# Seven pairs of steps instead of four, down products two steps behind, one of the block sums made by a transfer that adds

## What is computed

```python
def _swiglu(x, w_gate, w_up, w_down):
    return (jax.nn.silu(x @ w_gate) * (x @ w_up)) @ w_down

for l in range(2):
    x = x + 0.5 * _swiglu(_rmsnorm(x, ffn1_norm[l]), ffn1_w_gate[l], ffn1_w_up[l], ffn1_w_down[l])
    ...   # the mixer
    x = x + 0.5 * _swiglu(_rmsnorm(x, ffn2_norm[l]), ffn2_w_gate[l], ffn2_w_up[l], ffn2_w_down[l])
```

## Time and profile before

| | |
|---|---|
| runs, us | 1147.65, 1147.89, 1147.91 (median 1147.89) |
| the profiled execution | 1147.37 us, its span 1145.6 |
| granted TensorE clock | 0.999 of full speed |
| TensorE busy | 99% of the span |
| VectorE busy | 81% |
| ScalarE busy | 54% |
| POOL busy | 18% |

### The profile page before, as it was taken

One profiled execution on the slowest core, in us unless ns is written; L12 is line 12 of the kernel. 1 busy time (PEld: TensorE's weight loads), 2 busy tenths in 40 slices (PEclk: granted clock), 3 DMA queues, 4 the chain that ended last, 5 costly groups with the idle time before them and its releaser, 6 DMA issues.

```text
span 1145.6 us, 15668 instructions
## 1 busy us (share of the span) xinstructions
PE 1137.4 (99%) x5477; PEld 932.3 (81%) x5477; DVE 927.9 (81%) x1434; ACT 615.3 (54%) x789; POOL 211.7 (18%) x413
## 2 busy tenths in 40 slices
PE   9999999999999999999999999999999999999997
PEld 7888888888777888888888888888877788888886
DVE  6878886878987687789788788867898695988895
ACT  6455645457764454455454555454677635454453
POOL 2221230062000012121301221302510000122221
PEclk9999999999999999999999999999999999999999
DMA  8976575795325578756659756647953435886552
GB/s 296 312 265 209 165 232 167 239 263 193 125 75 184 184 233 268 260 164 223 205 194 298 256 175 224 207 154 216 274 164 108 141 136 183 284 283 217 162 196 103
DMA packets 168080, 235.82 MB, mean 206 GB/s; under 512 B 17376, under 2 KB 112848, under 8 KB 168016
## 3 DMA queue, kind: packets, MB, share of 16 engines
q1 hardware_dynamic: 146720, 222.23, 59.0%
q0 software_dynamic: 11008, 8.80, 3.2%
q10 hardware_dynamic: 10288, 4.00, 1.4%
HBM read 221.86 MB, written 1.05 MB: 195 GB/s over the span
## 4 chain that ended last, share of the span: by engine, by line
PE 99%; DVE 1%; issue 0%; ACT 0%; POOLq 0%; POOL 0%; DVEq 0%
PE ps L1645 28%; PE ps L1647 28%; PE ps L1646 28%; PE ps L1778 2%; PE ps L1779 2%; PE ps L1777 2%; PE ps L1903 2%; PE ps L1959 2%; PE ps L1931 2%; PE ps L1695 1%; PE ps L1664 1%; DVE wlo L639 0%; PE ps L1874 0%; PE ps L2082 0%; PE ps L1990 0%; PE ps L1950 0%
## 5 line engine op out<-in xcount | busy, mean ns | idle before, releaser
L639 DVE TENSOR_TENSOR wlo<-raw,whi 128x2048 fp32r<-128x2048 f32 (+2 forms) x195 | 427.5, 2198 | 80.5 <-ACT whi L1347 54.0
L1347 ACT ACTIVATE whi<-raw 128x2048 fp32r<-128x2048 f32 (+2 forms) x195 | 359.2, 1843 | 206.4 <-PE ps L1647 160.2
L1645 PE MATMUL ps<-whi,ht_hi 128*128 128x512 f32 (+1 forms) x1064 | 415.8, 391 | 0.6 <-DVE wlo L639 0.6
L1647 PE MATMUL ps<-whi,ht_lo 128*128 128x512 f32 (+1 forms) x1064 | 411.0, 386 | 0.0
L1646 PE MATMUL ps<-wlo,ht_hi 128*128 128x512 f32 (+1 forms) x1064 | 410.5, 386 | 0.0
L1645 PEld LDWEIGHTS ps<-whi,ht_hi 128*128 128x128 f32 x1064 | 199.9, 188 | 40.9 <-ACT whi L1347 1.0
L1647 PEld LDWEIGHTS ps<-whi,ht_lo 128*128 128x128 f32 x1064 | 199.8, 188 | 40.9
L1646 PEld LDWEIGHTS ps<-wlo,ht_hi 128*128 128x128 f32 x1064 | 200.1, 188 | 38.6
L536 POOL DMA_DIRECT2D act_blocks<-act_blocks x224 | 110.0, 499 | 458.0 <-DVE act_blocks L709 458.0
L1645 PE MATMUL ps<-whi,at_hi 128*128 128x512 f32 x304 | 118.5, 390 | 0.0
L1646 PE MATMUL ps<-wlo,at_hi 128*128 128x512 f32 x304 | 118.3, 389 | 0.0
(11 more groups left out here) (235 smaller groups left out, 1266.9 us busy)
## 6 DMA issues: line engine op xcount, KB each, us to landing
raw<-in_ffn_w_down_dram SPq DMA_DIRECT2D x88, 512.0 KB, 4.4
raw<-in_w_in_dram SPq DMA_DIRECT2D x88, 512.0 KB, 4.6
raw<-in_ffn_w_gate_dram SPq DMA_DIRECT2D x77, 512.0 KB, 4.0
raw<-in_ffn_w_up_dram SPq DMA_DIRECT2D x77, 512.0 KB, 5.0
T_raw<-in_ffn_w_gate_dram SPq DMA_DIRECT2D x16, 512.0 KB, 5.8
T_raw<-in_ffn_w_up_dram SPq DMA_DIRECT2D x16, 512.0 KB, 5.9
raw<-in_w_out_dram SPq DMA_DIRECT2D x16, 512.0 KB, 4.3
raw<-in_ffn_w_gate_dram SPq DMA_DIRECT2D x19, 256.0 KB, 2.9
```

Of the source, the lines that this page charges most:

```text
L639: nc.vector.tensor_tensor(wlo[:, n, 0:w], raw[:, n, 0:w], whi[:, n, 0:w].bitcast(F32), ALU.subtract).then_inc(lo_done, 1)
L1347: nc.scalar.activation(whi[:, n, 0:w], raw[:, n, 0:w], ACT.Copy).then_inc(hi_done, 1)
L1645: nc.tensor.matmul(o, xh, wh, start=start, stop=False)
L1647: return nc.tensor.matmul(o, xl, wh, start=False, stop=stop)
```

## The change

- **Pairs.** (0,0) has one pair, at step 8; the other three FFNs have two, at steps 4 and 8. An FFN's order of blocks is now made by `ffn_plan`: gate a, gate b of a step, then the down blocks of all steps up to two before it; a pair is b11, T2, b21, b22, T4 in the ring of blocks, and T3 and T1 from buffers of their own.
- **Two steps behind.** The down product of step i - 2 follows the gate blocks of step i. Activations alternate between at and bt, step banks between 0 and 2.
- **Sums.** T3, T1 and T2 are made by VectorE (`sum_of`), T4 by a transfer issued by POOL that adds T2 into T4's buffer (`add_part`). T2 and T4 are rounded straight into the ring (`convert_sum`). With p0 the FFN's first pair, T3 and T1 are summed in step p0 - 4 ahead of its products, T2 after them, together with `side_full`, which adds the halves of the normed x; `side_sums` (four instead of ten) follow in step p0 - 3. For a second pair the sums stand behind the first.
- **Turning.** Step 0 is turned as every other step. In steps 0 to 7 all twelve transfers are issued by POOL, and the four quadrants that stay are copied by ScalarE (`keep_act`) instead of transposed a second time by VectorE. PE's own turn of the first FFN is gone.
- **Loads.** The parts for the first pair are loaded with the blocks of steps p0 - 4 and p0 - 3; for the second with b22, 6a, 6b and down 2.
- **Loops** of PE and POOL are written out.

The core of the diff:

```diff
+PAIRED = {(0, 0): (8,), (0, 1): (4, 8), (1, 0): (4, 8), (1, 1): (4, 8)}
+def ffn_plan(l, f):
+    plan, waiting = [], []
+    for i, pair in ffn_steps(l, f):
+        if pair:
+            plan += [("b11", i), ("T2", i), ("b21", i), ("b22", i), ("T4", i)]
+            waiting += [i, i + 1]
+            continue
+        plan += [("gate", i, 0), ("gate", i, 1)] + [("down", j) for j in waiting if j <= i - 2]
+        waiting = [j for j in waiting if j > i - 2] + [i]
+    return plan + [("down", j) for j in waiting]
...
 # VectorE
+            def side_full(l, f):
+                nc.vector.tensor_tensor(full, ht_hi[:, :, :].bitcast(F32), ht_lo[:, :, :].bitcast(F32), ALU.add)\
+                    .then_inc(side_sum, 1)
...
+                nc.vector.tensor_tensor(sum_raw[name][:, :], sum_raw[first][:, :], sum_raw[second][:, :], ALU.subtract)\
+                    .then_inc(part_sub, 1)
...
+                p0 = PAIRED[l, f][0]
                 dve.wait_ge(rstd_ready, (l * 3 + n) * 3 + 3)
+                for n, key in enumerate(FFN_PLAN[l, f][:-2]):
+                    kind, i = key[:2]
+                    if kind == "b11":
+                        paired(l, f, i)
+                    if kind == "gate" and key[2] == 1:
+                        products(l, f, i)
+                        if l == f == i == 0:
+                            convert(l, s0 + 3)
+                        if not behind_pair(l, f, i):
+                            turn_product(l, f, i)
+                        convert_next(l, f, s0 + n + 3)
+                        if i == p0 - 4:
+                            sum_of(l, f, p0, "T2")
+                            side_full(l, f)
+                        if i + 2 in PAIRED[l, f][1:]:
+                            sum_of(l, f, i + 2, "T3")
+                    if kind == "gate" and key[2] == 0:
+                        if i and not behind_pair(l, f, i):
+                            convert_next(l, f, s0 + n + 3)
+                        if i == p0 - 4:
+                            sum_of(l, f, p0, "T3")
+                            sum_of(l, f, p0, "T1")
+                        if i == 2:
+                            act_rest(l, f, 0)
+                        if i == p0 - 3:
+                            side_sums(l, f)
+                        if i == p0 - 1:
+                            side_rest(l, f)
+                    if kind == "down":
+                        k = rounded_behind(l, f, i)
+                        if k == NSTEP - 1 or k == NSTEP - 2:
+                            act_rest(l, f, k)
+                        convert_next(l, f, s0 + n + 3)
+                        if k is not None and k < NSTEP - 2:
+                            act_rest(l, f, k)
...
 # POOL
+            def add_part(l, f, p):
+                z = PAIR_NUMBER[l, f, p]
+                pool.wait_ge(part_in["T4"], (z + 1) * 32)
+                pool.wait_ge(part_sub, z * 3 + 3)
+                apart(pool)
+                pool.dma_start(sum_raw["T4"][:, :], sum_raw["T2"][:, :], accum_op=ALU.add).then_inc(part_added, 16)
...
 # ScalarE
+            def keep_act(l, f, i):
+                eng.wait_ge(act_turned, (l * 2 + f) * NSTEP + i + 1)
+                blocks_in, blocks_out = act_set(i)
+                for q in range(4):
+                    nc.scalar.activation(blocks_out[32 * q:32 * q + 32, P * q:P * q + P],
+                                         blocks_in[32 * q:32 * q + 32, P * q:P * q + P], ACT.Copy)\
+                        .then_inc(act_kept_early, 1)
...
 # PE
+                product(1, quadrant(halves, 0, 0), from_ring(at("b11", p), 4), True).then_inc(slab_used, 1)
+                pe.wait_ge(side_l, r + 1)
+                product(0, s3, from_sums("T3"), True).then_inc(pair_ps, 1)
+                product(3, s2, from_ring(at("T2", p), 4), True).then_inc(slab_used, 1)
+                product(2, s1, from_sums("T1"), True).then_inc(pair_ps, 1)
...
-                with pe.Fori(2, PAIR) as i:
-                    gate_up(l, f, i)
-                    down(l, f, i - 1, (i, s0 + 1))
-                gate_up_pair(l, f)
+                for key in FFN_PLAN[l, f][4:-1]:
+                    kind, i = key[:2]
+                    if kind == "gate" and key[2] == 0:
+                        gate_up(l, f, i)
+                    if kind == "b11":
+                        gate_up_pair(l, f, i)
+                    if kind == "down":
+                        down(l, f, i)
```

More of the change, by code:

```diff
@@ L503, in direct, with behind_pair, pair_of, step_bank @@
[L503 to L508, removed]
+            return i == NSTEP - 1
+        def behind_pair(l, f, i):
+            return i - 2 in PAIRED[l, f]
+        def pair_of(l, f, i):
+            return next((p for p in PAIRED[l, f] if p <= i <= p + 1), None)
+        def step_bank(l, f, i):
+            return first_bank(f) if i == 0 else 0 if i % 2 else 2
@@ L547, in act_parts @@
         def act_parts(i):
-            if isinstance(i, int) and i == PAIR:
-                return [h[:, 0:2, :] for h in (bt_hi, bt_lo)]
             if final(i):
                 return [h[:, KD - 2:KD, :] for h in (ht_hi, ht_lo)]
-            return [h[:, :, :] for h in (at_hi, at_lo)]
+            return [h[:, :, :] for h in ((at_hi, at_lo) if i % 2 else (bt_hi, bt_lo))]
         def quadrant(parts, m, k):
@@ L1391, in act_round @@
                 wait_turned(eng, l, f, i)
[L1393 to L1396 removed]
+                if 1 < i < NSTEP - 1:
+                    wait_used(eng, l, SLAB_AT[l, f, "down", i - 2])
                 nc.scalar.activation(by_blocks(act_parts(i)[0]), turned_product(l, f, i), ACT.Copy).then_inc(ath, 1)
[L1399 to L1404 removed]
@@ L1807, in down @@
-            def down(l, f, i, s, start=False, between={}, order=range(4)):
+                pe.wait_ge(act_done, r * (2 * NSTEP) + p * 2)
+                product(1, quadrant(halves, 0, 0), from_ring(at("b11", p), 4), True).then_inc(slab_used, 1)
+                pe.wait_ge(side_l, r + 1)
+                product(0, s3, from_sums("T3"), True).then_inc(pair_ps, 1)
+                product(3, s2, from_ring(at("T2", p), 4), True).then_inc(slab_used, 1)
+                product(2, s1, from_sums("T1"), True).then_inc(pair_ps, 1)
@@ new lines, in gate_up_pair, with down @@
+                pe.wait_ge(pair_out, z * 2 + 1)
+                product(1, quadrant(halves, 0, 1), from_ring(at("b21", p), 4), False).then_inc(slab_used, 1)
+                pe.wait_ge(pair_out, z * 2 + 2)
+                product(2, s4, from_ring(at("b22", p), 4), False).then_inc(slab_used, 1)
+                pe.wait_ge(pair_sum, z * 5 + 2)
+                product(0, quadrant(halves, 1, 1), from_ring(at("T4", p), 4), False).then_inc(slab_used, 1)
+            def down(l, f, i, between={}, order=range(4)):
+                s = SLAB_AT[l, f, "down", i]
@@ L2135, in ffn @@
+                p0 = PAIRED[l, f][0]
+                parts = {("gate", p0 - 4, 0): (p0, "T1"), ("gate", p0 - 4, 1): (p0, "T3"),
+                         ("gate", p0 - 3, 0): (p0, "T2"), ("gate", p0 - 3, 1): (p0, "T4")}
+                for p, q in zip(PAIRED[l, f], PAIRED[l, f][1:]):
+                    parts["b22", p] = q, "T2"
+                    parts["gate", p + 2, 0] = q, "T3"
+                    parts["gate", p + 2, 1] = q, "T1"
+                    parts["down", p - 2] = q, "T4"
                 if l == f == 0:
```

678 lines of the change are left out of this document (325 added, 353 removed).

## The result

The changed kernel takes 1169.96 us, the median of four executions (1167.83 to 1170.11); the kernel before took 1147.79 beside it (1147.65 to 1147.91, four). The ratio is 1.019, with a 95% interval of 1.0177 to 1.0203: slower by 22 us. The forecast was 1152.8 with a range up to 1158. So the sign was right, and the size was wrong by 17 us.

The account below looks back on a forecast made before the run. PE's instruction count plus any new PE waits was taken as the bound: 1147.89 - 8.16 (matmuls) - 0.44 (transposes) + 13.5 (three head waits) = 1152.8 us, 0.4% slower, range 1139 to 1158.

Parts of the forecast that it names:

- What bounds the kernel: Whole kernel: PE's instruction count sets the end, plus any new PE wait; VectorE has least room, 14.60 of 15 us busy.
- What is removed from PE: Three more pairs take 8.16 us of gate/up matmuls off PE, and four transposes of the first FFN 0.44 us.
- What moves without a price: Later down products, POOL's crossings, ScalarE's copies and unrolled loops cost nothing; VectorE's average load fits, 1 us less in all.
- The head: Start of each FFN with a pair at step 4: VectorE's chain makes PE's down 0 wait 4.5 us, three times 13.5.
- The pair stretches: Around the seven pairs: everything in time with little room; cost 0, upper bound 0.5 us a pair, 3.5 us.
- What must be there for it: Loads at the heads: T2 lands near 395, 1b near 398, wanted at 410 and by 404; hidden by 6 us.
- T4's sum by transfer: T4's sum per pair: takes 2.2 us off VectorE; transfer hidden, cost 0, at most 11.6 us long by the rows.
- Rival 3: Pair stretches stall too, +0.5 us a pair, and d4 or d8 now and then: 1156.3, up to 1159 us; 18%.
- Rival 4: Blocks land late at the heads, 385 GB/s asked against 325 measured; 3 us late each gives 1161.8 us; 6%.

Follow-up runs that it names:

- run 1: The changed kernel without the three added pairs, one pair at step 8 in each FFN: 1148.33 us, ratio 1.0006 to the kernel before.
- Run 2: The changed kernel with full x and the four side sums moved behind the rest of activation 0 where the first pair is at step 4: 1157.17 us.
- run 3: The changed kernel with nineteen extra PE matmuls, results unread, ahead of down 0 in the three FFNs with a pair at step 4: 1161.06 us.
- run 8: The kernel before with three extra VectorE additions, results unused, ahead of the rest of activation 0 in three FFNs: 1167.68 us, ratio 1.0171.
- Run 4: The changed kernel with the second pair's raw parts T1 and T4 each loaded one block later: 1163.11 us, ratio 1.0139.
- Run 7: The change with later side sums, later second-pair loads and T1's rest ahead of b21's conversion, plus T4 summed by VectorE, not by transfer: 1155.74 us.
- run 9: The change with later side sums and later second-pair loads, plus T1's rest between b21's conversion and the rest of activation 2: 1146.04 us.

## Why the prediction was wrong

**What bounds the kernel** held: the loss is PE's waits and PE's clock, and nothing else that shows: these two and the removed work make 21.9 of the 22.8 us.

**What is removed from PE** held: 40 instructions, 8.6 us.

**What moves without a price** held: run 1 gives 1.0006 for all of it, with no more than 0.15% left by the interval.

**The head** held nearly to the step. The changed kernel's VectorE:

```profile
407.79 4.71 DVE L795 TENSOR_TENSOR T_raw<-T_raw 128x2048 f32<-128x2048 f32 x2
...
418.39 2.28 DVE L765 TENSOR_TENSOR sums_out<-ht_hi,ht_lo 128x2048 f32<-128x2048 f32 x1
...
426.92 2.25 DVE L678 TENSOR_TENSOR wlo<-raw,whi 128x2048 fp32r<-128x2048 f32 x1
430.37 2.29 DVE L678 TENSOR_TENSOR wlo<-raw,whi 128x2048 fp32r<-128x2048 f32 x1 [1.20 <-issue]
432.57 0.68 DVE L758 TENSOR_TENSOR bt_lo<-act_blocks,bt_hi 128x512 fp32r<-128x512 f32 x1
```

T3 at 407.9, full x at 418.4, down 0's block at 427.0 and the rest at 432.15 were written down; 407.79, 418.39, 426.92 and 432.57 came. The 0.4 us at the end is ScalarE's four copies, costed at 0.2 each, which take 1.31 together, 0.33 each, inside the bound of 0.38:

```profile
427.03 1.31 ACT L1479 ACTIVATE gated_all<-gated_all 32x128 f32<-32x128 f32 x4 [6.65 <-DVE gated_all L746]
```

4.5 us forecast, 4.6 of wait came, three times. Run 2 shows the chain as cause.

**The first step that failed: a wait was costed at its own length.** The sum had 3 x 4.5 = 13.5 for the heads, and no term for the rate at which PE works behind them. By the distances between starts this was worth 6.7 us at the heads and 1.7 at down 4 of (1,1); run 3, where all of it goes, is 8.9 us faster, and run 8 shows that it comes with the same wait in the kernel before. The rows of before have no such wait, since PE never waits there that long; but they also gave no ground for taking the rate of the earlier trace rows behind a wait, and an upper bound of half rate for some microseconds would have belonged in the range. The trace of before even shows the lower level once, at its end, where PE has had no work since 1139.3:

```profile
1143.30:1145.60 2.30, 0.00 (x0) 0.00 (x0) 0.00 (x0) 0.00 (x0) 0.00 (x0) 0.50 0.61 228
```

The Trainium skill has such a rule ("TensorE: Matmul & The Clock Gate", Part 1): the array's clock passes at half rate when the engine has been idle, and at the full one when it has been busy. The trace agrees, with 0.50 behind every wait of 4.6 us; which shorter waits did the same here stands below.

**The second: "The pair stretches", costed at 0 with a bound of 3.5 us.** The waits at down 4 are 1.56, 0.94 and 2.72 us, 5.2 together, 5.7 with their restarts, and the last brought 1.71 of half clock: 7.4 us, twice the bound. The rest of activation 4 was forecast at 495.1 for 495.7, 0.6 us in hand. In the trace both are later, and not by the same: PE asks at 499.70 - 1.56 = 498.14, 2.4 us behind the forecast (2.06 of it half clock behind the head, 0.3 the head's later restart), and the rest ends at 499.65, 4.5 us behind it. What I left out is the landing of down 2's block: the working followed when VectorE and ScalarE would be free for it and took it as loaded. "What must be there for it" was worked out for the head alone and not for the pair, where the second pair's parts stand in the same queue. The transfer engines were full there: 383 GB/s moved at a share of 1.06 between 470 and 478 of the changed kernel. Run 4 shows the late block as the cause. The bound failed for the same reason: slacks of 0.5 us bound a slip of the engines, not a late block that passes through silu, turn, twelve crossings and rounding.

**T4's sum by transfer**, costed at 0, held, and so did the bounds: it landed in 8.3 us (median of seven), under the 11.6 of the rows. The Trainium skill's figure ("DMA: Bandwidth & Descriptors", Bandwidth, measured), doubled, gave an estimate of 12.3; the measured 8.3 decides. Run 7 shows that the transfer is worth some 6 us in the form tried, of which the profiled run has some 3.4 as half clock.

**The rivals.** Rival 3, that the pair stretches stall too, came true in kind but was given at most 1159, since it too had no clock in it. Rival 4 (blocks late at the heads) did not happen there; late blocks happened at the pair instead. Its 325 GB/s was no ceiling either, as the 383 above show. With 14.2 us for the heads and 5.7 for down 4 the sum would have been 1147.89 - 8.6 + 19.9 = 1159.2; the clock's 8.4 makes it 1167.6, and some 2 us of small waits 1169.6.

**What stays open.** The (0,1) and (1,0) waits at down 4 differ (1.56 and 0.94) with the same instructions, and (1,1)'s is 2.72; nothing was tried that tells why. Why one wait of 2.05 us is followed by half clock and another of 2.06 or 2.16 us is not stays open too. The small waits left in run 9, 6.5 us by the distances between starts, are named in the waits only for 2.8; the rest are restarts and distances a little above 0.227, and were not taken apart. That a transfer which adds would stay hidden in the kernel before was not tried.

## What to carry to other kernels

When the engine that sets the end has no waits, price a new wait at its length and at what its rate is behind it: here 4.6 us cost 6.6, and a wait of 2 us cost its length in some places and 1.7 us more in others. Then follow a moved load through everything that stands behind it in its queue, and from the engine that waits for it to the last consumer: a block rounded 2.6 us later (478.85 for 476.27) became a wait of PE twenty microseconds on. And when the saving of a change (here 2.7 us a pair) is as small as single operations of an engine without slack, the place of one operation can decide its sign: three orders of the same instructions gave 1146.0, 1147.1 and 1149.8 us, of which the first two cannot be told apart and the third is slower than the kernel before.

## What the runs showed of the hardware

- PE's clock behind a wait. The waits of 2.72, 2.97 and 4.55 to 4.60 us were all followed by matmuls starting 0.43 us apart at 0.50, and none up to 1.93 us was. Around 2 us both happened: half clock behind 2.05 and 2.08 us (run 7, 452.54 and 1066.39), none behind 2.06 us twice in the same run, nor behind 2.16 us in runs 2 (496.52) and 3 (682.21). So the length of a wait alone does not decide it. The price varied for the same wait of 4.6 us: 2.06, 2.90 and 1.71 us. It is about half of the time that PE worked at half clock: 4.2, 6.0 and 3.4 us. In (0,1) and (1,0) the clock had fallen during the wait, in (1,1) it had not (a granted clock of 0.60, 0.91 and 1.00 in 430.0 to 433.3, 614.7 to 619.2 and 1009.6 to 1014.0); what sets that moment was not tried.
- Matmuls whose result nobody reads prevent it: with nineteen in the gap, the clock stayed at 1.00 behind all three heads, and the kernel was 8.9 us faster (run 3).
- A transfer that adds 1 MB from buffer to buffer costs POOL 0.98 us to issue and landed in 8.3 us. While the one of (0,1) ran, the transfer engines were 0.94 busy and moved 188 GB/s with the loads beside it; with loads alone they moved 383 GB/s at 1.06 (470 to 478). By this it takes more of the engines than its bytes say; what that costs the loads beside it no run shows:

```profile
420.70:428.90 8.20, 8.03 (x35) 6.12 (x33) 8.13 (x10) 1.77 (x5) 2.27 (x4) 1.00 0.94 188
```

- A ScalarE copy of 32x128 is 0.31 us long, and four in a row take 1.31; one of 64x256 is hardly longer (0.38).
